# Indexer scores handed over bank by bank, and four small moves in the first projections, in a two-part post-norm decoder layer

## What is computed

```python
rel = relu(einsum('bqhd,bsd->bqhs', iqb, ik) * (IDX_DIM ** -0.5))   # 4 indexer heads
score = einsum('bqh,bqhs->bqs', iwb, rel)                            # weighted sum over the heads
score = where(kpos <= qpos, score, NEG_INF)
_, idx = top_k(score, 256)
```

## Time and profile before

| | us |
|---|---|
| three runs | 2112.84, 2119.02, 2114.86 |
| their median | 2114.86 |
| the profiled execution, its own time | 2114.07 |
| its span on the core | 2112.3 |
| PE busy, by modelled ends | 2069.3 (98% of the span) |
| DVE, ACT, POOL busy | 1542.2, 973.8, 920.0 |

### The profile page before, as it was taken

One profiled execution on the slowest core, in us unless ns is written; L12 is line 12 of the kernel. 1 busy time (PEld: TensorE's weight loads), 2 busy tenths in 40 slices (PEclk: granted clock), 3 DMA queues, 4 the chain that ended last, 5 costly groups with the idle time before them and its releaser, 6 DMA issues.

```text
span 2112.3 us, 28918 instructions
## 1 busy us (share of the span) xinstructions
PE 2069.3 (98%) x10382; PEld 1725.8 (82%) x10382; DVE 1542.2 (73%) x2586; ACT 973.8 (46%) x1753; POOL 920.0 (44%) x724
## 2 busy tenths in 40 slices
PE   8999999999999999999999999999999999999998
PEld 7688888888888888888887888888788888888887
DVE  7658887776697666698785666677877777775668
ACT  4533333665624656615643656432433333344540
POOL 4187761333322232323322333533755656556651
PEclk9999999999999999999999999999999999999999
DMA  4133333101042111141031010341466665558862
GB/s 130 41 110 116 114 100 61 31 21 31 11 150 80 31 51 41 40 140 31 21 110 40 11 31 11 130 160 62 148 209 187 201 185 165 165 194 306 277 210 93
DMA packets 197374, 224.27 MB, mean 106 GB/s; under 512 B 25704, under 2 KB 149608, under 8 KB 197232
## 3 DMA queue, kind: packets, MB, share of 16 engines
q1 hardware_dynamic: 194320, 212.43, 32.5%
q10 hardware_dynamic: 2912, 10.00, 1.3%
HBM read 164.17 MB, written 58.23 MB: 105 GB/s over the span
## 4 chain that ended last, share of the span: by engine, by line
PE 81%; DVE 10%; ACT 3%; issue 3%; POOL 2%; DMA 1%; DVEq 0%; ACTq 0%; POOLq 0%
PE pair L1319 13%; PE pair L895 13%; PE pair L1185 7%; PE pair L879 6%; PE obank L1319 5%; PE obank L989 4%; PE chunk L968 4%; PE pair L1348 4%; PE pair L1278 3%; PE pair L940 3%; PE obank L1185 3%; PE pair L941 3%; PE chunk L1348 2%; PE obank L1348 2%; PE pair L1231 2%
## 5 line engine op out<-in xcount | busy, mean ns | idle before, releaser
L2126 POOL TENSOR_TENSOR w_lo<-w_raw,w_hi 128x1024 fp32r<-128x1024 f32 x64 | 158.2, 2472 | 323.3 <-ACT w_hi L1612 323.1
L2511 DVE TENSOR_TENSOR pt_lo<-chunk,pt_hi 128x512 fp32r<-128x512 f32 (+1 forms) x272 | 173.6, 639 | 86.3 <-ACT pt_hi L1635 82.6
L1635 ACT ACTIVATE pt_hi<-chunk 128x512 fp32r<-128x512 f32 (+1 forms) x272 | 150.8, 555 | 169.8 <-PE chunk L968 168.3
L2174 POOL TENSOR_SCALAR prob<-prob,att 128x256 f32<-128x256 f32 (+4 forms) x172 | 118.0, 696 | 232.8 <-DVE att L2447 232.8
L895 PE MATMUL pair<-act_hi,w_hi 128*128 128x512 f32 x432 | 187.2, 433 | 1.1 <-DVE heads L2452 0.9
L895 PE MATMUL pair<-act_hi,w_lo 128*128 128x512 f32 x432 | 170.7, 395 | 0.0
L895 PE MATMUL pair<-act_lo,w_hi 128*128 128x512 f32 x432 | 170.0, 394 | 0.0
L2329 DVE TENSOR_SCALAR_CACHE_REDUCE o_top<-score,stat 128x384 uint8<-128x384 f32 (+1 forms) x186 | 166.6, 941 | 0.4
L989 PE MATMUL obank<-pt_hi,heads 128*128 128x256 f32 (+1 forms) x568 | 148.3, 285 | 3.3 <-DVE o_t L2519 2.6
L1733 ACT ACTIVATE prob<-prob,att 128x256 f32<-128x256 f32 (+4 forms) x172 | 120.5, 701 | 44.5 <-DVE att L2435 42.9
L989 PE MATMUL obank<-pt_lo,heads 128*128 128x256 f32 (+1 forms) x568 | 138.6, 281 | 0.0
(11 more groups left out here) (487 smaller groups left out, 5931.5 us busy)
## 6 DMA issues: line engine op xcount, KB each, us to landing
down_sums<-dn_sums SPq DMA_DIRECT2D x40, 512.0 KB, 6.3
w_raw<-in_w_in SPq DMA_DIRECT2D x37, 512.0 KB, 3.9
gates<-o_t SPq DMA_DIRECT2D x22, 512.0 KB, 3.2
up_raw<-in_w_up SPq DMA_DIRECT2D x22, 512.0 KB, 4.8
gate_raw<-in_w_ffn_gate SPq DMA_DIRECT2D x22, 512.0 KB, 6.0
hidden<-gelu_s SPq DMA_DIRECT2D x22, 512.0 KB, 3.3
dn_raw<-down_sums SPq DMA_DIRECT2D x44, 256.0 KB, 4.1
h_in<-down_sums SPq DMA_DIRECT2D x44, 256.0 KB, 4.8
```

The lines of the kernel that those rows point to most:

```text
L2126: nc.gpsimd.tensor_tensor(split_into(1, g), w_raw[:, g % 2, 0:kt * cols], split_into(0, g).bitcast(F32), ALU.subtract).then_inc(lo_ready, 1)
L2511: nc.vector.tensor_tensor(pt_lo[:, n % PT_SLOTS, 0:m], t[:, 0:m], pt_hi[:, n % PT_SLOTS, 0:m].bitcast(F32), ALU.subtract).then_inc(chunk_f ...
```

## The change

1. **Scores by banks.** Units of up to 512 columns now take the two banks of `pair0` in turn. In wider units the first 512 columns (bank 0) and the rest (bank 1) are handed over apart: PE signals bank 0 by `bank_scored` and the unit's last by `pair_full`, ACT makes a relu for each bank, and PE waits, before it writes a bank, for the relu that last read this bank. PE's matmuls and their order are the same; ACT has 16 relus more. DVE's work is the same.
2. **Low parts first.** For the last two of the 16 blocks, DVE makes both low parts and then both sums. The low parts of blocks 8 to 15 raise a semaphore of their own, `x_low`, and PE's half 1 waits for 8 of these in place of `x_taken` 16.
3. **Forget rows.** The copy to `staged` moves from behind `pt_lo` to ahead of the sums of blocks 22 and 23; the end of `pt_lo` frees `pair0`. ACT waits for this copy before `pt_hi`, and makes its next weight split ahead of `pt_hi` and not behind it. The row of ones is set at the start of the program.
4. **Second weight split.** ACT splits the second weight tile right behind the first, ahead of block 8's high part.

```diff
+IDX_UNITS = [(i, h) for i in range(FIRST_TOPK, NTOK) for h in range(IDX_HEADS)]
+IDX_BANKS = [[n % 2] if (i + 1) * P <= 512 else [0, 1] for n, (i, h) in enumerate(IDX_UNITS)]
+RELUS = list(itertools.accumulate(len(banks) for banks in IDX_BANKS))
...
-                    pe.wait_ge(x_taken, 2 * NTOK)
+                    pe.wait_ge(x_low, NTOK)
...
-                            if n >= 1:
-                                pe.wait_ge(relu_done, n)
-                            stacked_scores(0, iq_t[:, h, i * P:(i + 1) * P], ik_hi, ik_lo, (i + 1) * P,
-                                           beside=n + 1)
...
+                        for (s, m), bank in zip(pieces((i + 1) * P), IDX_BANKS[n]):
+                            if bank in bank_read:
+                                pe.wait_ge(relu_done, bank_read[bank])
+                            at = bank * HALF
+                            nc.tensor.matmul(dst[:, at:at + m], iq_t[:, h, i * P:(i + 1) * P], ik_hi[:, s:s + m],
+                                             start=True, stop=False)
...
+                            if bank != IDX_BANKS[n][-1]:
+                                last.then_inc(bank_scored, 1)
+                            bank_read[bank] = RELUS[n] - (bank != IDX_BANKS[n][-1])
+                        last.then_inc(pair_full[0], 1)
...
-                        if n in (7, 8):
-                            split_weights()
+                        if n == 7:
+                            split_weights(2)
...
+                    if kind == "ik_f_iw":
+                        ahead()
+                        act.wait_ge(rows_staged, 1)
                     for r in range(2):
                         part(hi[r * HD:(r + 1) * HD, :], src[0:HD, :])
-                    ahead()
+                    if kind == "kv_c":
+                        ahead()
...
-                            nc.scalar.activation(prob[:, unit % 2, 0:n], src[:, 0:n], ACT.Relu).then_inc(relu_done, 1)
...
+                            nc.scalar.activation(prob[:, unit % 2, s:s + m], pair[0][:, bank * HALF:bank * HALF + m],
+                                                 ACT.Relu).then_inc(relu_done, 1)
...
-                own(nc.vector.memset(ones, 1.0))
...
+            own(nc.vector.memset(bias[F_ROWS, :], 1.0))
...
+                        low.then_inc(x_taken if t < 4 else x_low, 1)
+                        for m in {2 * NTOK - 2: (), 2 * NTOK - 1: (n - 1, n)}.get(n, (n,)) if t >= 4 else ():
...
+                        if n == 3 * NTOK - 2:
+                            nc.vector.tensor_copy(staged, pair_in(0)[:, :]).then_inc(rows_staged, 1)
...
-                            dve.wait_ge(relu_done, unit + 1)
+                            dve.wait_ge(relu_done, RELUS[unit])
```

More of the change, by code:

```diff
@@ L513, in build_layer @@
         half_free = sem("half_free")
+        bank_scored = sem("bank_scored")
         relu_done = sem("relu_done")
@@ L1906, in _ @@
                 elif kind == "scores":
[L1907 to L1913, removed]
-                            else:
-                                act.wait_ge(pair_free[0], tiles[0].n - 2)
-                            nc.scalar.activation(prob[:, unit % 2, 0:n], src[:, 0:n], ACT.Relu).then_inc(relu_done, 1)
-                            if 0 <= unit - XS_FIRST < 4:
-                                x_sums_hi(4, unit - XS_FIRST)
-                            if unit == LAST_EARLY_SPLIT - 1:
-                                take_filler(0, pair[1], bias)
-                            elif unit == LAST_EARLY_SPLIT:
-                                ahead()
+                    banks = Tally()
+                    for unit, (i, h) in enumerate(IDX_UNITS):
+                        tiles[0].next()
+                        if unit < 2:
+                            act.wait_ge(c_stored, 16)
+                        else:
+                            act.wait_ge(pair_free[0], tiles[0].n - 2)
+                        for (s, m), bank in zip(pieces((i + 1) * P), IDX_BANKS[unit]):
+                            if bank != IDX_BANKS[unit][-1]:
+                                act.wait_ge(bank_scored, banks.next())
+                            else:
+                                act.wait_ge(pair_full[0], tiles[0].n)
+                            nc.scalar.activation(prob[:, unit % 2, s:s + m], pair[0][:, bank * HALF:bank * HALF + m],
+                                                 ACT.Relu).then_inc(relu_done, 1)
+                        if 0 <= unit - XS_FIRST < 4:
+                            x_sums_hi(4, unit - XS_FIRST)
+                        if unit == LAST_EARLY_SPLIT - 1:
+                            take_filler(0, pair[1], bias)
+                        elif unit == LAST_EARLY_SPLIT:
+                            ahead()
                 elif kind == "gates":
@@ L2789, in _ @@
                     k = kind == "kv_c"
-                    src = pair_in(k)
+                    src = pair_in(1) if k else pair[0]
                     hi, lo = (heads[:, 2, :], heads[:, 3, :]) if k else (ik_hi, ik_lo)
                     for r in range(2):
-                        lo_part(lo[r * HD:(r + 1) * HD, :], src[0:HD, :], hi[r * HD:(r + 1) * HD, :], 2 * (1 - r))
-                    nc.vector.tensor_copy(staged, src[:, :]).then_inc(pair_free[k], 1)
+                        last = lo_part(lo[r * HD:(r + 1) * HD, :], src[0:HD, :], hi[r * HD:(r + 1) * HD, :], 2 * (1 - r))
+                    if k:
+                        last = nc.vector.tensor_copy(staged, src[:, :])
+                    last.then_inc(pair_free[k], 1)
                     if kind == "ik_f_iw":
```

31 lines of the change are left out of this document (17 added, 14 removed).

## The result

The changed kernel takes 2107.42 us, the median of 7 runs (2104.39 to 2110.65). The kernel before, timed beside it, takes 2117.19, the median of 7 (2112.84 to 2121.88). The ratio is 0.9946, with a 95% interval of 0.9934 to 0.9957. The forecast was 2103.2 (2099.5 to 2109.0): the time lies in the range, 4.2 us above the likeliest value and above the band (2101.5 to 2105.0) that was given 0.55. The profiled execution took 2109.34, span 2107.5.

The account below looks back on a forecast made before the run. After 115.39 us PE is busy 1965.6 of 1996.6 us, so the gain is how much earlier it enters the gates. Front 3.0 plus scores 7.9 make 10.9 us off 2114.07: 2103.2 (range 2099.5 to 2109).

Parts of the forecast that it names:

- Scores: Scores stage: 147 matmuls at 0.227 us plus small waits make about 34.8 us against 42.66, 7.9 saved (4.1 to 9.2).
- The loop through one bank: Scores: bank 0 to the next unit's bank 0 takes 1.32 us, deciding only at 640 columns, by 0.07 for two units.
- rival 1: Scores: halves keep PE waiting, a restart per wide unit, only 4.1 us saved: 2107.0, or 2108.5 with weak front; chance 0.14.
- PE's own work per unit: Scores: matmuls plus one filler part take 1.59 us at 1024 columns, 1.48 at 896, 1.36 at 768, 1.25 at 640.
- The wait kept at 0.8: Scores, after unit 11: ACT makes a sigmoid and issues a store ahead of the next relu; PE still waits 0.8 us.
- Front: Stretch ahead of the scores: shorter waits of PE let the scores start 3.0 us sooner (bounds 1.5 to 3.6).
- Early split and low parts first: Ahead of half 1: PE goes on at 27.75 in place of 29.05, 1.3 us saved with POOL first, 1.9 with DVE first.
- The forget rows: Ahead of the scores: moving the copy removes PE's 0.7 us wait and shrinks its 1.6 us wait for `iq_t` to 0.6.
- Rival 3: Clock elsewhere: a 1.2 GHz stretch of 3.4 us vanishes (2099.8) or comes twice (2106.6); chance 0.14, split evenly.
- rival 2: Front gives 1.5 us or less because DVE and POOL fall badly in two places: 2104.7 to 2106; chance 0.10.
- rival 4: Slower: further 1.2 GHz stretches cost 3.4 us each, gain gone from the fourth, six give 2123.6; chance 0.02.
- rival 5: Scores: banks do nothing because something other than the relu holds PE, front gain only, 2111.1; chance 0.05.

Follow-up runs that it names:

- before_again: The kernel before, unchanged, run for a second trace: 2117.51 us.
- scores_only: The kernel before with part 1 of the change alone (scores and relu by bank): 2109.97 us, ratio 0.9968.
- front_only: The changed kernel with the old scores and relu, so parts 2 to 4 alone: 2112.72 us, ratio 0.998.
- after_again: The changed kernel, unchanged, run for a second trace: 2109.01 us.
- after_more: The changed kernel, unchanged, timed beside the others: 2108.66 us, ratio 0.9946.
- late_split: The changed kernel with the second weight split put back behind block 8: 2106.13 us, ratio 0.9951.
- no_forget: The changed kernel with the copy to `staged` back behind `pt_lo` and ACT's weight split behind `pt_hi`; first score matmul at 60.04 us, total time not given.
- even_banks: The changed kernel with units wider than 512 columns cut in two equal halves: scores stage 34.81 us, total time not given.
- sums_spread: The changed kernel with two of DVE's four `early_gates` sums moved behind blocks 12 and 14: 2108.9 us, ratio 0.9944.
- pool_late: The changed kernel with four POOL memsets of 0.2 us ahead of the third `w_lo` that holds DVE: 2105.29 us, ratio 0.9929.
- pool_late3: The changed kernel with four POOL memsets of 0.2 us ahead of each of three `w_lo` that hold DVE: 2102.5 us, ratio 0.9916.
- best: The changed kernel with both the equal halves of even_banks and the memsets of pool_late3: 2102.24 us, ratio 0.9917.

## Why the prediction was right, and where its size was off

First gate product, "held" (DVE's small operations of over 1 us near the merge of B), PE's wait for `mid` there, and the time lost at 1.2 GHz behind the first gate product (half the length of such stretches, from the record of the granted clock). The remainder is the span from the first gate product to the end, less the wait and this loss:

| kernel | first gate product | from there to the end | held | wait | clock | remainder |
|---|---|---|---|---|---|---|
| before | 115.23 | 1997.0 | 2 | 1.2 | 3.4 | 1992.4 |
| before_again | 115.35 | 2000.4 | 3 | 3.5 | 5.1 | 1991.8 |
| scores_only | 109.09 | 2001.0 | 3 | 3.5 | 6.8 | 1990.7 |
| front_only | 111.92 | 1998.5 | 2 | 0.9 | 5.1 | 1992.5 |
| changed | 105.33 | 2002.2 | 3 | 3.9 | 6.8 | 1991.5 |
| after_again | 104.58 | 2002.6 | 3 | 3.5 | 6.8 | 1992.3 |
| after_more | 105.60 | 2003.9 | 3 | 3.5 | 8.5 | 1991.9 |
| late_split | 104.93 | 2002.6 | 3 | 3.5 | 8.5 | 1990.6 |
| no_forget | 106.42 | 2003.8 | 3 | 3.9 | 8.5 | 1991.4 |
| even_banks | 103.79 | 2002.9 | 3 | 3.9 | 6.8 | 1992.2 |
| sums_spread | 105.24 | 1999.2 | 2 | 1.1 | 6.8 | 1991.3 |
| pool_late | 105.15 | 2000.7 | 2 | 1.7 | 6.8 | 1992.2 |
| pool_late3 | 104.81 | 1995.6 | 1 | 0 | 3.4 | 1992.2 |
| best | 103.72 | 1995.4 | 1 | 0 | 3.4 | 1992.0 |

The way to the end varies by 8.5 us between kernels that have the same program there; the remainder varies by 1.9. So two things make up most of it: the wait at the merge of B, and the clock. They are tied: in all eight traces in which PE waited 3.5 us or more, a stretch at 1.2 GHz followed it, and in none of the other six.

Point by point:

- **Scores, 7.9 forecast, 7.3 measured.** The loop through one bank was right: one wait is left, units of 1024 columns are 1.60 to 1.62 apart, and rival 1 (a restart per wide unit) did not come. The step that failed in size is "PE's own work per unit", counted by columns alone: a pair of 128 columns costs 0.17 + 0.06 where 0.11 was counted, and the loop took 0.11 at 640 columns and not 0.07. `even_banks` removes this and 0.2 of the wait, and takes 34.6 by the forecast's marks. The wait kept at 0.8 was 0.5, which hid a part of the miss.
- **Front, 3.0 forecast, 3.5 at full clock.** In the second trace of the changed kernel half 1 starts at 27.73 (forecast 27.75), the second `iq` tile has no wait, the filler is at 54.75 (55.1), the first gate product at 104.58 (near 104.5). POOL was first at the second `w_lo`, as taken, though by an earlier landing of the weight and not by the 0.1 us that was forecast. The Trainium skill, "SBUF — State Buffer", section "SBUF: two separate sides", says that of the two engines the one that starts first has the shared ports for its whole instruction; four sums at 7.0 us with two `w_lo` beside them and 4.9 with one agree. Early split and low parts first were put at 1.3 together; half 1 starts 1.4 sooner behind the first product, 0.1 of it from the early split (`late_split`). The forget rows were put at 1.7 and gave 2.0 (`no_forget`).
- **The sum, 10.9 forecast.** Up to the first gate product, both at full clock there, 115.23 and 115.35 before stand against 104.58: 10.7. In the profiled pair only 9.9, since the changed kernel's execution fell to 1.2 GHz in its first 20 us. By the timed ratio 11.4 us (2117.19 x 0.0054), by the medians beside the result 9.8, by those beside `after_more` 12.3 (2120.95 and 2108.66).
- **The base.** Of the 4.2 us 3.1 come from the step that takes the sum "off the profiled execution's 2114.07", with the median "0.8 above that execution"; the other 1.1 are 9.8 saved in place of 10.9, less than the medians can tell. That execution was a fast one of its kernel: medians of 7, 19, 9 and 9 runs are 2117.19, 2117.2, 2119.69 and 2120.95. It had two held operations where a second trace had three. 2117.2 - 10.9 would have been 2106.3. That the range held is in part luck: by the number alone 2107.42 is rival 1's time (2107.0 to 2108.5), and the marks show that rival 1 did not come.
- **Rival 3** was right as a mechanism. The record of the clock shows 13.6 us at 1.2 GHz behind the first gate product in the changed kernel, in three stretches, where before there was one of 6.8. It was priced at 3.4 per further stretch, which is right for one of 6.8 us; those of 3.4 us cost 1.7. What was missing from the list is the wait at the merge of B. The forecast was to fail if "a stretch behind 105 us changes its length", and this is the one, though it changes in the kernel before too. No rival and no chance stood for it, though DVE's held operations are in the trace before.
- **Rivals 1, 2, 4, 5** did not come.

What stays open: why the clock falls at some thin places of branch D in one execution and not in another, and why it fell in the first 20 us in five of the fourteen traces, with the front of before (`scores_only`) as with the new one. What part 2 is worth alone wasn't tested.

## What to carry to other kernels

Read what an edit saves between its own marks, and add it to a base taken from several runs, not from the one profiled execution; where the trace has short operations that now and then take the full length of another engine's, look for a place where one more or less changes a wait. When a tile is handed over in parts, try equal parts: here a narrow rest cost PE more than its columns and left the wide part's consumer the longer one. A kernel can be faster with one of its producers started 1 us late, if that lets a chain of short operations through.

## What the runs showed of the hardware

- An operation of DVE on 6 numbers per partition takes 0.17 us, and 1.55 to 2.40 where it starts up to 0.9 us behind a subtraction of POOL that takes 2.4; the two end together. It holds for `TENSOR_SCALAR` with one input in SBUF and for `SCALAR_TENSOR_TENSOR` with two. The same operations beside POOL's memsets take 0.17. The Trainium skill, "SBUF — State Buffer", section "SBUF: two separate sides", has a VectorE operation with two SBUF inputs blocked only against a GpSimd operation that reads SBUF. `SCALAR_TENSOR_TENSOR` at 0.17 beside the memset, which reads nothing, agrees.
- The held operations repeat: 10.3 and 9.3 us apart in the changed kernel, and POOL's `w_lo` 10.4 and 9.2 apart. So each time DVE's step ends where the next `w_lo` starts. `pool_late3` breaks the row: from 598.63 on all are free, and the steps take 7.1 and 8.2 us.
- Two matmuls of 128 columns in a row take 0.17 us, and the 512-column one behind them is followed after 0.29; four of 320 columns take 0.57, their columns' time.
- A wait of 3.5 us or more for `mid` was followed by 3.4 us at 1.2 GHz in eight of eight traces, one of 0.9 to 1.7 in none of four.
